# Where the softmax scale is applied: two attention stages that take a negated maximum of queries scaled beforehand

## The reference, cut to what matters

```python
# first block: 8 heads, each with two maps (c) of 64 features; lam is one number
q = rope(q) * 64 ** -0.5
s = einsum('bqhcd,bkhcd->bhcqk', qb, k)
s = where(allowed, s, -inf)          # a query sees the keys of its own 64-chunk and of earlier ones
p = softmax(s)
a = p[:, :, 0] - lam * p[:, :, 1]
o = einsum('bhqk,bkhe->bqhe', a, v)

# mixed layer, latent attention: 8 heads, 64 features without and 32 with rotation
# the same mask and softmax, scale 96 ** -0.5, one map per head, 64 value features
```

## Time and profile before

| what | value |
|---|---|
| median of 3 runs | 4095.99 us (4093.35 to 4112.11) |
| profiled execution, its own time | 4100.22 us |
| its span in the trace | 4098.4 us |
| PE busy | 3673.0 us, 90% of the span |
| DVE, ACT, POOL busy | 1622.0, 1089.9, 1140.8 us |
| attention of the first block in the trace | about 380 to 765 us |
| attentions of the mixed layers | about 3083 to 3250 and 3803 to 3976 us |

### The profile page before, as it was taken

How to read it: one execution, slowest core, us unless ns; L and a number is a source line. 1 busy time by engine, 2 the same in 40 slices (tenths; PEclk the granted TensorE clock), 3 DMA queues, 4 the chain that set the end, 5 groups by cost and what they waited for, 6 DMA issues and landing times. The chain is left out here.

```text
span 4098.4 us, 44490 instructions
## 1 busy us (share of the span) xinstructions
PE 3673.0 (90%) x17688; PEld 2844.7 (69%) x17688; DVE 1622.0 (40%) x2113; ACT 1089.9 (27%) x1622; POOL 1140.8 (28%) x672
## 2 busy tenths in 40 slices
PE   6995777799999999999999999599978979997897
PEld 5874455588888888878888888387635658764565
DVE  2122666531112136953111212544735531373563
ACT  2001665310101012732010101113435411343450
POOL 3221442133333334633333333222301121230111
PEclk9997878899999999999999999699988989998898
DMA  2122331011111122121111111213023120202221
GB/s 101 51 79 81 113 108 57 31 51 47 46 50 48 46 69 72 44 88 47 46 51 46 46 51 46 77 33 97 31 78 93 57 103 27 77 32 77 78 72 57
DMA packets 74265, 256.63 MB, mean 63 GB/s; under 512 B 8944, under 2 KB 10128, under 8 KB 74128
## 3 DMA queue, kind: packets, MB, share of 16 engines
q1 hardware_dynamic: 53312, 187.11, 14.6%
q10 hardware_dynamic: 13904, 42.49, 3.0%
q0 software_dynamic: 6912, 25.17, 1.9%
HBM read 207.28 MB, written 43.25 MB: 61 GB/s over the span
## 5 line engine op out<-in xcount | busy, mean ns | idle before, releaser
L1119 POOL CAST tk_w_hi<-tk_w_raw 128x1024 fp32r<-128x1024 f32 x160 | 178.6, 1116 | 1185.8 <-PE tk_acc L191 547.7
L191 PE MATMUL tk_acc<-tk_b_hi,tk_w_hi 128*128 128x512 f32 x1280 | 397.3, 392 | 10.4 <-POOL tk_w_lo L1121 10.4
L191 PE MATMUL tk_acc<-tk_a_hi,tk_w_hi 128*128 128x512 f32 x1280 | 398.2, 392 | 3.4 <-POOL tk_w_lo L1121 3.4
L191 PE MATMUL tk_acc<-tk_b_lo,tk_w_hi 128*128 128x512 f32 x1280 | 398.2, 393 | 0.0
L191 PE MATMUL tk_acc<-tk_b_hi,tk_w_lo 128*128 128x512 f32 x1280 | 398.0, 392 | 0.0
L191 PE MATMUL tk_acc<-tk_a_lo,tk_w_hi 128*128 128x512 f32 x1280 | 397.8, 392 | 0.0
L1121 POOL TENSOR_TENSOR tk_w_lo<-tk_w_raw,tk_w_hi 128x1024 fp32r<-128x1024 f32 x160 | 394.2, 2464 | 12.8
L191 PE MATMUL tk_acc<-tk_a_hi,tk_w_lo 128*128 128x512 f32 x1280 | 397.4, 392 | 0.0
L1266 ACT ACTIVATE tk_sq<-tk_r 128x1024 f32<-128x1024 f32 x64 | 67.9, 1060 | 1078.9 <-DVE tk_r L1384 1078.9
L1359 DVE TENSOR_TENSOR xT<-tk_acc,xT 128x1024 f32<-128x1024 f32 x80 | 98.0, 1225 | 616.9 <-PE tk_acc L191 616.9
L191 PEld LDWEIGHTS tk_acc<-tk_b_hi,tk_w_hi 128*128 128x128 f32 x1280 | 241.0, 188 | 63.5 <-POOL tk_w_lo L1121 10.8
(11 more groups left out here) (368 smaller groups left out, 6680.3 us busy)
## 6 DMA issues: line engine op xcount, KB each, us to landing
tk_w_raw<-in_w_trunk SPq DMA_DIRECT2D x160, 512.0 KB, 3.5
da_w_mod<-in_ada_w POOLq DMA_DIRECT2D x48, 512.0 KB, 3.8
pj_w_raw<-in_w_in SPq DMA_DIRECT2D x44, 512.0 KB, 3.6
qk_w_raw<-in_w_qkv SPq DMA_DIRECT2D x24, 512.0 KB, 3.6
x_dram<-xT ACTq DMA_DIRECT2D x24, 512.0 KB, 5.9
qk_dram<-qk_o ACTq DMA_DIRECT2D x16, 512.0 KB
ma_w_raw<-in_w_out SPq DMA_DIRECT2D x16, 512.0 KB, 4.1
xT<-x_dram SPq DMA_DIRECT2D x16, 512.0 KB, 8.2
```

Source lines behind the costliest of these rows:

```text
L191: last = pe.matmul(self.acc[:, u, s * HALF:(s + 1) * HALF], w[:, u, k, :], h[:, k, s * HALF:(s + 1) * HALF], start=(k == order[0] and part ...
L1119: pool.tensor_copy(pn.hi[:, u, :, :], pn.raw[:, u, :, :]).then_inc(sems[f"w_hi{u}"], 1)
```

## The change

The scores' PSUM now holds values that already carry the scale: the queries are scaled when they are written to DRAM. In both attentions the maximum is written negated by the reduction itself, into the slot that the exponential reads as its bias, so the 128x1 multiplication, its wait and the semaphore `max` are gone, and the exponential has the scale 1.0. In `qkv_rope` the four products of each turn become `scalar_tensor_tensor` with a constant, 64 ** -0.5 for the four turns of queries and 1.0 for the four turns of keys, which makes two hardware loops of four turns out of one of eight. In `mla_project` ACT's copy becomes an ACTIVATE Copy with a constant scale, 96 ** -0.5 for the six query products and 1.0 for the four of keys.

```diff
@@ qkv_rope, DVE
-                    with dve.Fori(n_v, n_v + 8) as i:
-                        a, b = pn.acc[:, 0, :], pn.acc[:, 1, :]
-                        pn.wait_sums(dve, 0, i)
-                        pn.wait_sums(dve, 1, i)
-                        dve.tensor_tensor(t[:, 0, :], a, cos[:, :], ALU.mult)
-                        dve.tensor_tensor(t[:, 2, :], a, sin[:, :], ALU.mult).then_inc(sems["psum_free0"], 1)
-                        dve.tensor_tensor(t[:, 1, :], b, sin[:, :], ALU.mult)
-                        dve.tensor_tensor(t[:, 3, :], b, cos[:, :], ALU.mult).then_inc(sems["psum_free1"], 1)
...
+                    for first, scale in ((n_v, 64 ** -0.5), (n_v + 4, 1.0)):
+                        with dve.Fori(first, first + 4) as i:
+                            a, b = pn.acc[:, 0, :], pn.acc[:, 1, :]
+                            pn.wait_sums(dve, 0, i)
+                            pn.wait_sums(dve, 1, i)
+                            dve.scalar_tensor_tensor(t[:, 0, :], a, scale, cos[:, :], ALU.mult, ALU.mult)
+                            dve.scalar_tensor_tensor(t[:, 2, :], a, scale, sin[:, :], ALU.mult, ALU.mult)\
+                                .then_inc(sems["psum_free0"], 1)
+                            dve.scalar_tensor_tensor(t[:, 1, :], b, scale, sin[:, :], ALU.mult, ALU.mult)
+                            dve.scalar_tensor_tensor(t[:, 3, :], b, scale, cos[:, :], ALU.mult, ALU.mult)\
+                                .then_inc(sems["psum_free1"], 1)
...
@@ attention, DVE
-                        dve.tensor_reduce(st[:, t % 4, 0, m:m + 1], sc[:, m, 0:parts, 0:w], axis=AXXY, op=ALU.max)\
-                            .then_inc(sems["max"], 1)
-                        dve.wait_ge(sems["max"], 2 * t + m + 1)
-                        dve.tensor_scalar(st[:, t % 4, 1, m:m + 1], st[:, t % 4, 0, m:m + 1], -scale, None,
-                                          ALU.mult).then_inc(sems["neg"], 1)
+                        dve.tensor_reduce(st[:, t % 4, 1, m:m + 1], sc[:, m, 0:parts, 0:w], axis=AXXY, op=ALU.max,
+                                          negate=True).then_inc(sems["neg"], 1)
@@ attention, ACT
-                                       ACT.Exp, bias=st[:, t % 4, 1, m:m + 1], scale=scale,
+                                       ACT.Exp, bias=st[:, t % 4, 1, m:m + 1], scale=1.0,
@@ mla_project, ACT
-                        act.copy(ab[:, 0, at, :] if at < 2 else o[:, at % 2, :], acc[:, at % 2, :])\
-                            .then_inc(sems["out"], 1)
+                        act.activation(ab[:, 0, at, :] if at < 2 else o[:, at % 2, :], acc[:, at % 2, :], ACT.Copy,
+                                       scale=96 ** -0.5 if order[at] < 6 else 1.0).then_inc(sems["out"], 1)
```

More of the change, by code:

```diff
@@ L686, in _ @@
                     dve.sem_inc(sems["rot"], n_v)
-                    with dve.Fori(n_v, n_v + 8) as i:
-                        a, b = pn.acc[:, 0, :], pn.acc[:, 1, :]
-                        pn.wait_sums(dve, 0, i)
-                        pn.wait_sums(dve, 1, i)
-                        dve.tensor_tensor(t[:, 0, :], a, cos[:, :], ALU.mult)
-                        dve.tensor_tensor(t[:, 2, :], a, sin[:, :], ALU.mult).then_inc(sems["psum_free0"], 1)
-                        dve.tensor_tensor(t[:, 1, :], b, sin[:, :], ALU.mult)
-                        dve.tensor_tensor(t[:, 3, :], b, cos[:, :], ALU.mult).then_inc(sems["psum_free1"], 1)
[L695 to L699, removed]
+                    for first, scale in ((n_v, 64 ** -0.5), (n_v + 4, 1.0)):
[9 more added lines that the diff above has]
+                                .then_inc(sems["psum_free1"], 1)
+                            dve.wait_ge(sems["psum_free1"], i + 2)
+                            dve.wait_ge(sems["stored"], 32 * i + (16 - 32 * n_v))
+                            dve.tensor_tensor(o[:, 0, :], t[:, 0, :], t[:, 1, :], ALU.subtract)
+                            dve.tensor_tensor(o[:, 1, :], t[:, 3, :], t[:, 2, :], ALU.add).then_inc(sems["rot"], 1)
+                            dve.wait_ge(sems["rot"], i + 1)
     def diff_lambda(self, neg_lam):
@@ L739, in attention @@
         nc = self.nc
-        names = ["landed0", "landed1", "scores", "neg", "max", "exp", "prob", "pt", "pts", "pv", "nat", "ot",
+        names = ["landed0", "landed1", "scores", "neg", "exp", "prob", "pt", "pts", "pv", "nat", "ot",
                  "out", "link", "mask", "nat_sq", "nat_sum", "nat_root", "nat_normed", "silu", "mod_scaled", "mod_added", "mod_used"] + \
@@ L2178, in mixed_back @@
         names = PANEL_SEMS + [
-            "landed0", "landed1", "scores", "max", "neg", "exp", "prob", "pt", "pts", "pv", "out", "link", "mask",
+            "landed0", "landed1", "scores", "neg", "exp", "prob", "pt", "pts", "pv", "out", "link", "mask",
             "z_in0", "z_in1", "gated", "o_hi", "o_lo", "s_hi", "s_lo", "x_sq", "acc"] + [f"x_ld{n}" for n in range(DK)]
@@ L2348, in maximum @@
                         dve.wait_ge(sems["scores"], i + 1)
-                        dve.tensor_reduce(st[:, t % 4, 0, m:m + 1], score(m, parts, w), axis=AXXY, op=ALU.max)\
-                            .then_inc(sems["max"], 1)
-                        dve.wait_ge(sems["max"], i + 1)
-                        dve.tensor_scalar(st[:, t % 4, 1, m:m + 1], st[:, t % 4, 0, m:m + 1], -scale, None, ALU.mult)\
-                            .then_inc(sems["neg"], 1)
+                        dve.tensor_reduce(st[:, t % 4, 1, m:m + 1], score(m, parts, w), axis=AXXY, op=ALU.max,
+                                          negate=True).then_inc(sems["neg"], 1)
                     def normalise(t, m):
```

## The result

The changed kernel takes **4064.63 us** (median of 6 runs, 4058.84 to 4067.37) against 4095.51 (6 runs, 4093.35 to 4112.11): a ratio of 0.9916, 95% interval 0.9899 to 0.9934, 31 us less by the medians and 34 by the ratio. That is faster by more than 0.5%, where "within 0.5%" was held the likeliest and 18 us were forecast. The time lies just inside the range.

The account below looks back on a forecast made before the run. The first block's attention was taken as a loop of latencies, the mixed ones as bound by TensorE. Terms -16.2, -2 and +0.2 us made -18 us, from the median 4096.0 to 4078.0 us, range 4063 to 4090.

Parts of the forecast that it names:

- The ring: First block's attention, loop of scores, maxima, negations and exponentials: dropping the negations and their waits was to save 16.2 us.
- The output copy in the 768 block: First attention: VectorE's copy, waiting for TensorE's values, stands before the reciprocal, so only 0.20 of 0.34 us go.
- the 512 block's gain: First attention: 0.28 us, still counted because the next maximum stands behind a norm's sum that waits for ScalarE's square.
- The overlap of two unwaited instructions: VectorE in the first attention: two instructions with no wait between them overlap by about 0.08 us.
- The negated maximum: Both attentions: the maximum with its sign turned was taken to be as long as the plain maximum.
- the scaled queries: Projections: scaling of queries and keys taken as 0, at most 1 us; in the latent projection +0.2 us.
- That rival (5%): Negated maximum dearer: kernel slower from 0.14 us more per reduction, 4125 us at half a length more; chance 0.05.
- The mixed attentions: Mixed layers' attentions, TensorE nearly full: only its idle time behind VectorE can go, 0 to 4.4 us, taken as -2.
- The step that failed: First attention, 128 block: VectorE waits 4.94 us for values that TensorE makes behind eight sum matmuls, so no gain.
- less arrives: First attention, 512 block: VectorE's multiply-add falls behind POOL's addition, 9.5 us back, 4087.5 us; chance 0.23.
- the clock rises: First attention: TensorE idles less, some score stretches get 2.4 GHz, 8 us more gained, 4070 us; chance 0.22.
- the prediction's own signs of being wrong: New profile: among them, a clock in 380 to 740 us that differs by more than 0.03 from before.

Follow-up runs that it names:

- the first experiment: Changed kernel with the maximum plain again and a separate 128x1 multiplication by -1 with its wait in both attentions, scaled queries kept: 4098.41 us, ratio 1.0005.

## Why the prediction was right and wrong

**The ring: right.** 16.2 us were worked out, 17 measured in steps at equal clock. The output copy in the 768 block takes back what was said (the next step gains 0.17 us, 0.14 worked out), the 512 block's gain arrives through the norm's square in units 2 to 6 (0.24 and 0.23) and not in units 7 and 8, which the prediction did not tell apart, and the 128 block's own step gains nothing.

**The overlap of two unwaited instructions: right.** Two maxima take 2.09 us at 896 columns, where one behind the other would take 2.18. The Trainium skill ("VectorE: DVE Perf Modes", section "The DRAIN you can't avoid") says that a semaphore behind each VectorE instruction costs nothing extra; the traces speak against that, with 0.04 us behind the end where there is a wait and 0.08 or 0.09 before it where there is none. The same section of the Trainium skill adds, and the prediction left out, that "A next op that is not held starts earlier"; with this the trace agrees.

**The negated maximum, the scaled queries: right.** 1086 and 415 ns, as the plain ones; 1225 for 1224 ns; 12 ns a copy on ScalarE. That rival (5%) is out by the rows and by the first experiment.

**The mixed attentions: undecided.** -2 us were taken; the scatter of the stage is larger.

**The step that failed** is the sentence "In the 128 block VectorE waits 4.94 us for the values, which TensorE makes behind the eight sum matmuls: no gain". The wait was right, but I took it as a fixed length. It ends with eight matmuls that are 3.41 or 1.84 us long, and it ends just in front of an addition on POOL that catches VectorE or does not. Both turned: 4.94 us became 3.70, 1.79 became 0.35, and the term taken as 0 measured 8.7 us by the medians, 9 to 12 by all readings. The clock's part outside this step, 6 to 7 us, was also left out of the sum and stood only among the rivals.

**The rival "less arrives"** named the right mechanism and the wrong block and sign. In the 512 block the order held as its margin said: the multiply-add still starts 0.10 us ahead of POOL's addition (0.12 worked out). It can turn: in the sixth unit of the first experiment VectorE and POOL show

```profile
631.72 2.93 DVE L948 SCALAR_TENSOR_TENSOR da_pr<-da_pr,da_st 128x512 f32<-128x512 f32 x1
...
631.77 2.34 POOL L832 TENSOR_TENSOR da_mod_acc<-da_mod_acc,da_w_mod 128x1024 f32<-128x1024 f32 x1 [3.40 <-ACT da_w_mod L1030]
```

2.93 us where it takes 0.75 elsewhere, the loss that the prediction had worked out. The collision of which the prediction said "this trace shows no such turn" was in that trace, one block further on: a 128 column scaling of 1.79 us. Reading the group of line 944 by width, a mean of 1258 ns at 128 columns, would have shown it; I had read only starts and waits there.

**The rival "the clock rises"** (22%, 4070 us) is nearest to what happened: 0.79 to 0.87. But it priced only the scores, and it held against itself that "the idle time that precedes these blocks, the 4.94 us in the 128 block, stays". That idle time is in part made of the eight matmuls at 1.2 GHz, so it fell when they ran at 2.4. The clock's parts outside the fifth step were 6 to 7 us, near the 8 that the rival gave. A clock more than 0.03 from before was also one of the prediction's own signs of being wrong.

**Luck.** That 4064.63 us still lies in the stated range of 4063 to 4090 us is luck: the range's lower end was set by the clock's gain on the scores, and what brought the time there was for the larger part a term taken as 0.

**What stays open** is why, with a ring shorter by 0.3 us a block, the clock falls behind the matmuls in units 3 to 6 and no longer ahead of them. That their length follows the moment of the fall is shown, with map 1's negation, idle matmuls elsewhere in the unit and between units of one run; which stretch of TensorE's work sets that moment was not isolated. Nor is it always for the better: in the changed kernel's second unit the matmuls took 2.63 us where before had 1.84, and its fifth step was 7.0 us instead of 4.35. The first unit varied between 36 and 51 us over the profiled executions of all kernels; that this is much of the spread of the runs is likely and not shown.

## What to carry to other kernels

An operation on a 128x1 result that stands between two engines in a latency ring, with its wait, costs more than its own 0.15 us: the two of a block came to 0.24 to 0.42 us where the gain arrived, and that can be worked out from the timeline of one block. But read every instruction of such a ring by its shape, and ask of each that is longer than its kind what held it: a 128 column scaling of 1.8 us says that another engine had started first, and a small shift will change that by whole microseconds in either direction. Price small matmuls in a loop of latencies at both clocks, 3.41 and 1.84 us here, and put them where nothing waits behind them: here that brought 16 us without the change.

## What the runs showed of the hardware that was not expected

- Sixteen PE instructions of one column (eight products) take 3.41 us at 1.2 GHz and 1.84 at 2.4; lengths between (2.2 to 3.3 us) appear where the granted clock falls under them.
- The start order of a 2.33 us addition on POOL and a VectorE instruction within some tenths of a microsecond decided 1.3 to 2.1 us. Where VectorE was first POOL paid instead: its addition took 3.33 us, the 1.23 us product started 0.11 us ahead of it.
- Two groups of nine idle matmuls, ahead of the scores of the 640 and the 896 block, brought the 896 block's from 3.36 to 1.77 us; the first group took 3.74 us itself, at a granted clock of 0.54, the second 2.17 at 1.00.
